# An encoder layer on one core: the Strassen-type down product in visits of half the K-chunks, with its loads and stores spread over three queues

## The chip, the cores and the metric

The program runs on one core of a Trainium2 chip. The metric is the device time of one execution in microseconds; of several executions the median is taken. One more execution was taken with the hardware profiler, and every duration below comes from that one.

## What is computed

One encoder layer is applied to a prompt of 512 rows and a sample of 2,048 rows (2,560 rows of 1,024 floats in the kernel, 20 tiles of 128 rows). The part that matters here is the end of the layer: the gated MLP with its convolution, and the last layer norm.

```python
def conv_gated_mlp(x, w_up, conv_w, conv_b, w_down):
    h = x @ w_up
    ...
    h = h_prev * conv_w[0] + h * conv_w[1] + h_next * conv_w[2] + conv_b
    a, gate = jnp.split(h, 2, axis=-1)
    return (jax.nn.silu(gate) * a) @ w_down

def encoder_trunk(...):
    ...
        x = layer_norm(DEEPNORM_ALPHA * x + mix, ln1_g[l], ln1_b[l])
        f = conv_gated_mlp(x, w_up[l], conv_w[l], conv_b[l], w_down[l])
        x = layer_norm(DEEPNORM_ALPHA * x + f, ln2_g[l], ln2_b[l])
    return x
```

D_FF is 2,816, that is 22 chunks of 128 along the K axis of the down product. Everything is float32; a matrix product is done in three passes over operands that are split into a high and a low part.

## The kernel before, in words

The program has three parts: `project_gla` (names with `front_`), `natten` (`near_`) and `trunk`. The change is in `trunk`, whose own stages follow each other on TensorE: the output projection with the first norm, the up product, and the down product with the last norm. Every engine runs its own list of instructions in order, and a wait on a semaphore holds all that stands behind it on that engine. SyncE (SP) does nothing but ask for DMAs.

**Up product.** It is a Strassen-type product: seven products stand for eight block products. There are 126 steps: six passes over the chunks of W_up (four passes of four lanes, then two of three), in each three blocks of the sequence, in each the seven products. A step is a `phase(n)` of TensorE: four loads of the x operand (`xop`) by every lane, 48 matmuls with four lanes and 36 with three. The result of a lane lies in a PSUM bank, which the step after the next uses again. VectorE reads the banks of products 1, 3, 4, 5, 6 (`take`, L2432), ScalarE those of products 0 and 2 (L2224). In the first steps of each group of seven VectorE also does the convolution of the group before (`convolve_lane`, L2443 and L2450, two lanes a step), ScalarE the centre tap and the silu (L2234, L2241), and GpSimd the product and the store of the gated block g to `g_s` (L2127, L2130).

**The operands of W_down** are made on the way. `CHUNK_TAGS` names for each of 11 chunks (each a pair of K-chunks) the step in which it begins. SyncE loads four quarters of W_down (L1913); in three steps (three, two and two of seven) ScalarE and VectorE write the seven combinations, high half (`emit_hi`, L2264) and low half (`emit_lo`, L2472), into one of two buffers in `trunk_s`, and SyncE stores them to `wop` (`store_emit`, L1918), one after each of its x loads in the step (L1942). GpSimd makes the sums that the combinations need (`combine_down`, L2108 to L2118). The two buffers are the place in which GpSimd also puts a sum of W_up for the next pass (`sum_w`, L2090, L2092); it therefore waits there until all stores of the chunk have landed, and SyncE's loads of the next W_up quarters wait for that sum.

**Down product.** The 20 row tiles are ten pairs; five pairs are one half of the work. A half has seven phases, one for each of the seven products (`DOWN_A`), and in each phase every pair (lane) is visited once: 70 visits in all, each 11 K-chunks of three matmuls with 512 columns, 33 matmuls into the bank of that lane. The right operand of a phase is 11 units of `wop`, 512 KB each, in a ring of 15 (`load_w`, L1951). Its unit comes free when the last lane of the phase has used it, so 15 units mean: the 11 of this phase and 4 of the next. The left operand of a visit is made of blocks of g (704 KB each, rows of 512 bytes; `load_raw`, L1970): one block for most products, three for the product `s2`; `visit_combine` (VectorE, L2484, L2486, L2490) adds or subtracts them, `visit_hi` (ScalarE, L2273) and `visit_lo` (VectorE, L2494) split the result. After a visit VectorE adds the bank to the output rows (`visit_take`, L2507, L2511), and in the last two phases it norms a tile in each visit (`down_norm`, L2521 to L2531; GpSimd stores it, L2161). The rows of x that the result is added to are asked for by `load_rows` (L1979).

All loads of the down product stand in SyncE's list, in the order of the visits:

```python
for v in range(NVISIT):
    while loaded < len(raws) and raws[loaded][0] <= v + 3:
        load_raw(loaded)
        ...
    if v % DLANES == DLANES - 1:
        first = KH * (v // DLANES) + WUNITS
        for u in range(first, min(first + KH, DHALVES * PHASES * KH)):
            load_w(u)
```

and each `load_w` waits there until the last lane has used the unit whose place it takes.

## Time and profile before

| | us |
|---|---|
| median of 3 runs | 3243.07 |
| lowest and highest | 3231.84, 3245.0 |
| the profiled execution, its own time | 3248.93 |
| its span, first to last instruction | 3247.1 |

The span of the profile is 1.8 us shorter than the execution's own time. TensorE is busy for 93% of it, VectorE for 62%, ScalarE for 34%, GpSimd for 22%. A matmul's end is modelled in the profile, so a busy TensorE is not a TensorE at its peak: the number of matmuls in a stretch, times the time that one takes where nothing waits, tells more than the busy time. The DMA share is the mean busy share of the 16 DMA engines; it can come out a little above 1.

### The profile page before, as it was taken

How to read it: one execution, taken by the hardware profiler on the slowest of the kernel's cores; microseconds unless marked ns; L12 is line 12 of the kernel's file. 1: busy time of each engine (PE TensorE's matmuls, PEld its weight loads, DVE VectorE, ACT ScalarE, POOL GpSimd, SP SyncE). 2: the span in 40 equal slices, each digit the busy share in tenths (PEclk: the TensorE clock that was granted, in tenths of full speed). 3: DMA queues.
4: the chain of work that ended last, by engine and by line, in shares of the span. 5: the costliest groups of instructions: out<-in, count | busy, mean ns of one | idle time of the engine just before them, and what ended most of it. 6: DMA issues, size and time to landing. Idle time of an engine off the chain costs nothing.

```text
span 3247.1 us, 42991 instructions
## 1 busy us (share of the span) xinstructions
PE 3016.5 (93%) x15590; PEld 2547.6 (78%) x15590; DVE 2024.5 (62%) x3237; ACT 1102.2 (34%) x2019; POOL 706.1 (22%) x626
## 2 busy tenths in 40 slices
PE   6999999896999998999999999999989988999897
PEld 5777767664777777888899999999879876777685
DVE  7637646743766765668577575775656644466438
ACT  2257346521443442224243332433333321212111
POOL 0012111005445400422333243332333210000000
PEclk9999999987999999999999999999999989999998
DMA  7889788947887766998888888898899989879884
GB/s 279 319 280 305 247 279 264 293 157 256 271 269 234 261 202 207 319 318 296 292 263 314 305 299 308 268 317 303 299 336 355 341 308 302 273 259 335 281 254 148
DMA packets 498946, 910.18 MB, mean 280 GB/s; under 512 B 39952, under 2 KB 274592, under 8 KB 498736
## 3 DMA queue, kind: packets, MB, share of 16 engines
q1 hardware_dynamic: 486096, 854.39, 78.8%
q0 software_dynamic: 12640, 53.04, 4.4%
q8 instruction: 126, 2.06, 0.3%
q14 instruction: 84, 0.69, 0.1%
HBM read 695.85 MB, written 215.55 MB: 281 GB/s over the span
## 4 chain that ended last, share of the span: by engine, by line
PE 36%; DMA 12%; DVE 9%; issue 2%; POOL 1%; ACT 1%; SPq 1%; POOLq 0%; DVEq 0%; ACTq 0%
PE trunk_ps L76 12%; PE trunk_ps L77 12%; PE trunk_ps L78 12%; DMA wop<-trunk_s 3%; DMA shared_spare<-g_s 3%; DMA shared_ring<-xop 2%; DMA trunk_x1t<-g_s 2%; DVE trunk_tt L2443 2%; DVE trunk_tt L2450 1%; DVE shared_ring L2494 1%; DVE trunk_s L2472 1%; DVE trunk_x1t L2484 1%; DVE trunk_x1t L2486 1%; DVE trunk_h L2358 0%; SPq L1970 0%
## 5 line engine op out<-in xcount | busy, mean ns | idle before, releaser
L76 PE MATMUL trunk_ps<-shared_ring 128*128 128x512 f32 (+2 forms) x1202 | 456.5, 380 | 27.5 <-DVE shared_ring L2494 9.3
L77 PE MATMUL trunk_ps<-shared_ring 128*128 128x512 f32 (+2 forms) x1202 | 450.6, 375 | 0.0
L78 PE MATMUL trunk_ps<-shared_ring 128*128 128x512 f32 (+2 forms) x1202 | 448.9, 373 | 0.0
L76 PEld LDWEIGHTS trunk_ps<-shared_ring 128*128 128x128 f32 x1202 | 228.6, 190 | 67.5 <-DMA shared_ring<-wop 16.8
L76 PE MATMUL front_acc<-shared_ring 128*128 128x512 f32 x640 | 260.8, 407 | 8.1 <-ACT front_out L578 8.1
L76 PE MATMUL trunk_ps<-shared_ring,trunk_w_more 128*128 128x426 f32 (+1 forms) x648 | 237.8, 367 | 30.4 <-DMA shared_ring<-xop 30.4
L77 PE MATMUL front_acc<-shared_ring 128*128 128x512 f32 x640 | 252.8, 395 | 0.0
L78 PE MATMUL front_acc<-shared_ring 128*128 128x512 f32 x640 | 252.6, 395 | 0.0
L78 PEld LDWEIGHTS trunk_ps<-shared_ring 128*128 128x128 f32 x1202 | 229.3, 191 | 26.0
L77 PEld LDWEIGHTS trunk_ps<-shared_ring 128*128 128x128 f32 x1202 | 229.2, 191 | 23.8
L76 PE MATMUL trunk_ps<-trunk_w_rest,shared_ring 128*128 128x512 f32 x560 | 223.1, 398 | 25.2 <-DMA trunk_w_rest<-wop 15.3
L77 PE MATMUL trunk_ps<-shared_ring,trunk_w_more 128*128 128x426 f32 (+1 forms) x648 | 236.7, 365 | 0.0
L78 PE MATMUL trunk_ps<-shared_ring,trunk_w_more 128*128 128x426 f32 (+1 forms) x648 | 235.1, 363 | 0.0
L78 PE MATMUL trunk_ps<-trunk_w_rest,shared_ring 128*128 128x512 f32 x560 | 221.5, 396 | 0.0
L77 PE MATMUL trunk_ps<-trunk_w_rest,shared_ring 128*128 128x512 f32 x560 | 221.3, 395 | 0.0
L2127 POOL TENSOR_TENSOR trunk_h<-trunk_tt 128x851 f32<-128x851 f32 (+2 forms) x66 | 130.1, 1971 | 408.1 <-DVE trunk_h L2457 184.7
L2234 ACT ACTIVATE trunk_tt<-trunk_h,trunk_cw 128x851 f32<-128x851 f32 (+2 forms) x132 | 136.4, 1095 | 211.0 <-DVE trunk_h L2432 184.1
L2443 DVE SCALAR_TENSOR_TENSOR trunk_tt<-trunk_h,trunk_cw,trunk_tt 128x851 f32<-128x851 f32 (+3 forms) x176 | 202.0, 1199 | 5.6 <-ACT trunk_tt L2234 4.7
L76 PE MATMUL trunk_ps<-shared_ring,trunk_w_rest 128*128 128x426 f32 (+1 forms) x528 | 191.0, 362 | 12.5 <-DMA shared_ring<-xop 6.9
L77 PE MATMUL trunk_ps<-shared_ring,trunk_w_rest 128*128 128x426 f32 (+1 forms) x528 | 191.3, 362 | 0.0
L78 PE MATMUL trunk_ps<-shared_ring,trunk_w_rest 128*128 128x426 f32 (+1 forms) x528 | 190.0, 360 | 0.0
L2432 DVE TENSOR_TENSOR trunk_h<-trunk_ps,trunk_p 128x426 f32<-128x426 f32 (+1 forms) x198 | 110.6, 598 | 98.1 <-PE trunk_ps L78 97.2
(252 smaller groups left out, 6237.6 us busy)
## 6 DMA issues: line engine op xcount, KB each, us to landing
shared_ring<-xt_s SPq DMA_DIRECT2D x280, 512.0 KB, 6.3
shared_ring<-xop SPq DMA_DIRECT2D x312, 426.0 KB, 5.7
shared_ring<-xop SPq DMA_DIRECT2D x168, 428.0 KB, 5.6
shared_spare<-in_w_up SPq DMA_DIRECT2D x198, 256.0 KB, 5.5
trunk_w_rest<-wop SPq DMA_DIRECT2D x80, 512.0 KB, 8.4
wop<-trunk_s SPq DMA_DIRECT2D x77, 512.0 KB, 5.3
shared_ring<-wop SPq DMA_DIRECT2D x74, 512.0 KB, 9.4
shared_spare<-g_s SPq DMA_DIRECT2D x46, 704.0 KB, 10.2
```

The source lines that it names most:

```text
L76: pe.matmul(out, lh, rh, start=first, stop=False, skip_group_check=skip)
L77: pe.matmul(out, lh, rl, start=False, stop=False, skip_group_check=skip)
L78: return pe.matmul(out, ll, rh, start=False, stop=last, skip_group_check=skip)
L2127: pool.tensor_tensor(part, tt[:, k % 2, 0, 0:n], tt[:, k % 2, 1, 0:n], ALU.mult).then_inc(g_done, 1)
L2234: act.activation(tt[:, k % 2, f, 0:n], h[:, l, f, c:c + n], ACT.Identity, bias=tap[:, 3:4], scale=tap[:, 1:2]).then_inc(tt_done, 1)
L2432: dve.tensor_tensor(out, src, other, ALU.add).then_inc(dve_read, 1)
L2443: ins = dve.scalar_tensor_tensor(out, h[:, l, f, c - 1 + a:c - 1 + b], taps[f][:, 0:1], out, ALU.mult, ALU.add)
L2450: ins = dve.scalar_tensor_tensor(out, h[:, l, f, c + 1 + a:c + 1 + b], taps[f][:, 2:3], out, ALU.mult, ALU.add)
L2472: dve.tensor_tensor(out[:, HALF:D].bitcast(F32R), quad_of(quad_no), out[:, 0:HALF], ALU.subtract).then_inc(wd_lo, 1)
L2484: dve.tensor_tensor(total, raw_a(own[0]), raw_a(own[1]), ALU.add).then_inc(a_comb, 1)
L2486: dve.tensor_tensor(total, total, raw_a(own[2]), ALU.subtract).then_inc(a_comb, 1)
L2494: dve.tensor_tensor(a_buf(v)[:, 1], a_source(v), a_buf(v)[:, 0].bitcast(F32), ALU.subtract).then_inc(a_lo, 1)
```

## The change

A visit is cut in two: the first covers six K-chunks (`KSPAN`), the second five. All five lanes do their first visit, then all five their second; the bank of each lane stays open in between. There are 140 visits, of 18 and of 15 matmuls. A half block of g is 384 or 320 KB; the buffers for it are eight halves in place of four whole ones, and those for the split operand six halves in place of three whole ones. For `a11` both blocks of the first row are loaded and their difference is left in the lane's sum, so that `s2` needs one block more and not three: eight blocks a pair in place of nine.

SyncE's list keeps the loads of x, of W_up, of W_down and of `wop`, and the g halves of the first ten visits; `load_raw` for later visits is in ScalarE's list, `load_rows` in GpSimd's, and `store_emit` in ScalarE's. The chunks that began in steps 9, 30, 51, 72, 93 and 114 begin one step sooner.

```diff
-CHUNK_TAGS = (9, 25, 30, 46, 51, 67, 72, 88, 93, 109, 114)
-DLANES, DHALVES, WUNITS, ABUFS, RAWA = 5, 2, 15, 3, 4
+CHUNK_TAGS = (8, 25, 29, 46, 50, 67, 71, 88, 92, 109, 113)
+KSPAN = ((0, 6), (6, 11))
+DLANES, DHALVES, WUNITS, ABUFS, RAWA = 5, 2, 15, 6, 8
...
-        blocks = {"a11": ((0, 0),), "a12": ((1, 0),), "s2": ((0, 1), (1, 1), (0, 0)), "s3": ((1, 1),), "a22": ((1, 1),),
+        blocks = {"a11": ((0, 0), (0, 1)), "a12": ((1, 0),), "s2": ((1, 1),), "s3": ((1, 1),), "a22": ((1, 1),),
                   "s1": ((0, 0),), "s4": ((1, 0),)}[op]
...
         @block.sync
...
-                    if 1 <= j <= len(emits_at(n)):
-                        store_emit(emits_at(n)[j - 1])
...
+            for r in range(4, RAWA):
+                load_raw(sp, r)
+            for r in range(RAWA, raws_by_sync):
+                load_raw(sp, r)
+            for u in range(WUNITS, DHALVES * PHASES * KH):
+                load_w(u)
...
         @block.gpsimd
             for n in range(NSTEP_UP + 3):
+                c, step = chunk_step(n)
+                if n == NSTEP_UP:
+                    for i in range(2):
+                        pool.wait_ge(wd_stored[i], 16 * len(range(i, PHASES * KH, 2)))
+                    load_rows(pool, 0, 0)
+                    pool.wait_ge(dve_read, len(dve_no))
+                    load_rows(pool, 0, 1)
+                if c is not None:
+                    combine_down(c, step)
                 products(n)
...
-                c, step = chunk_step(n)
-                if c is not None:
-                    combine_down(c, step)
...
+            for l in range(2, DLANES):
+                load_rows(pool, 0, l)
...
         @block.scalar
+            def store_emit(number):
+                c, e, _, out = emit_of(number)
+                act.wait_ge(wd_lo, number + 1)
+                act.dma_start(wop[DOWN_W.index(EMITS[e]), c], out).then_inc(wd_stored[number % 2], 16)
+
+            def emits(n):
+                numbers = emits_at(n)
+                for j, number in enumerate(numbers):
+                    emit_hi(number)
+                    if j:
+                        store_emit(number - 1)
+                if numbers:
+                    store_emit(numbers[-1])
...
             for v in range(1, NVISIT + 1):
-                if 3 <= v + 2 < NVISIT:
-                    visit_hi(v + 2)
+                if 8 <= v + 5 < NVISIT:
+                    visit_hi(v + 5)
+                while loaded < len(raws) and raws[loaded][0] <= v + 10 and raws[loaded - RAWA][0] <= v + 3:
+                    load_raw(act, loaded)
+                    loaded += 1
...
         @block.vector
+            take(NSTEP_UP - 1)
+            visit_combine(0)
+            visit_combine(1)
+            visit_lo(2)
+            visit_lo(3)
+            visit_combine(2)
+            visit_combine(3)
+            convolve_lane(LAST_S, 0)
+            visit_lo(4)
+            visit_combine(4)
+            convolve_lane(LAST_S, 1)
...
             for v in range(1, NVISIT + 1):
-                if 3 <= v + 2 < NVISIT:
-                    visit_lo(v + 2)
+                if 8 <= v + 5 < NVISIT:
+                    visit_lo(v + 5)
                 visit_take(v - 1)
-                if v + 3 < NVISIT:
-                    visit_combine(v + 3)
+                if 7 <= v + 6 < NVISIT:
+                    visit_combine(v + 6)
...
         @block.tensor
-                for k in range(KH):
-                    u = KH * (v // DLANES) + k
+                k0, k1 = KSPAN[g]
+                for k in range(k0, k1):
+                    u = KH * (v // PER_PHASE) + k
```

**First place: SyncE around the first chunk of W_down.** The rows are DMA requests in the order of SyncE's list; `wop<-trunk_s` is a store of a W_down operand, `shared_ring<-xop` loads of x for the up product, `shared_spare<-in_w_up` quarters of W_up. Before:

```order
L1918 DMA wop<-trunk_s 128x1024
L1942 DMA shared_ring<-xop 128x852 x3
L1913 DMA shared_spare<-in_w_up 128x512 x6
L1918 DMA wop<-trunk_s 128x1024
L1942 DMA shared_ring<-xop 128x852
L1918 DMA wop<-trunk_s 128x1024
L1942 DMA shared_ring<-xop 128x852 x3
L1913 DMA shared_spare<-in_w_up 128x512 x6
```

With the change, the same stretch from the load of the four W_down quarters on:

```order
L1966 DMA shared_spare<-in_w_down 128x512 x4
L1990 DMA shared_ring<-xop 128x852 x16
L1966 DMA shared_spare<-in_w_up 128x512 x6
L1990 DMA shared_ring<-xop 128x852 x4
L1966 DMA shared_spare<-in_w_up 128x512 x6
```

The stores are gone from SyncE's list; between the quarters of W_down and the first six of W_up now stand 16 loads of x, that is four steps.

**Second place: VectorE around the same chunk.** L2457 (L2500 with the change) ends a lane of the convolution, `trunk_s<-shared_spare,trunk_s` writes the low half of a W_down operand, and `trunk_h<-trunk_ps,trunk_p` reads four banks of a step. Before:

```order
L2450 SCALAR_TENSOR_TENSOR trunk_tt<-trunk_h,trunk_cw,trunk_tt 128x851 x2
L2457 COPY trunk_h<-trunk_h 128x2x2
L2432 TENSOR_TENSOR trunk_h<-trunk_ps,trunk_p 128x426 x4
L2472 TENSOR_TENSOR trunk_s<-shared_spare,trunk_s 128x512 x5
L2432 TENSOR_TENSOR trunk_h<-trunk_ps,trunk_p 128x426 x4
L2472 TENSOR_TENSOR trunk_s<-shared_spare,trunk_s 128x512 x2
```

With the change:

```order
L2493 SCALAR_TENSOR_TENSOR trunk_tt<-trunk_h,trunk_cw,trunk_tt 128x851 x2
L2500 COPY trunk_h<-trunk_h 128x2x2
L2515 TENSOR_TENSOR trunk_s<-shared_spare,trunk_s 128x512 x3
L2475 TENSOR_TENSOR trunk_h<-trunk_ps,trunk_p 128x426 x4
L2515 TENSOR_TENSOR trunk_s<-shared_spare,trunk_s 128x512 x4
L2475 TENSOR_TENSOR trunk_h<-trunk_ps,trunk_p 128x426 x4
```

Three low halves have moved ahead of the read of the four banks that follows the convolution.

**Third place: the requests of the down product.** `g_s` is the gated block, `wop` the operands of W_down. Before, all in SyncE's list:

```order
L1951 DMA trunk_w_rest<-wop 128x1024 x4
L1951 DMA shared_ring<-wop 128x1024 x7
L1970 DMA trunk_x1t<-g_s 128x11x128
L1970 DMA shared_spare<-g_s 128x11x128 x2
L1970 DMA trunk_x1t<-g_s 128x11x128 x2
```

With the change, in ScalarE's list, between the high halves of the left operand:

```order
L2302 ACTIVATE shared_ring<-shared_spare 128x640
L1901 DMA trunk_x1t<-g_s 128x6x128 x2
L2302 ACTIVATE shared_ring<-trunk_x1t 128x768
L1901 DMA shared_spare<-g_s 128x6x128
L1901 DMA shared_spare<-g_s 128x5x128
```

SyncE's list has only loads of `wop` after the first ten visits' g, and ScalarE asks for g one or two halves at a time.

## Rows read from the trace of the kernel before

**Rows 1.** The page, its head.
```profile
span 3247.1 us, 42991 instructions
```

**Rows 2.** Busy time by stretch, up product; columns stand in the first line.
```profile
core 0: us, PE busy (x) PEld busy (x) DVE busy (x) ACT busy (x) POOL busy (x), PEclk, DMA share, GB/s
...
1598.10:1624.60 26.50, 21.20 (x98) 19.77 (x98) 5.00 (x9) 2.25 (x3) 10.17 (x8) 0.88 0.86 307
1624.60:1802.70 178.10, 178.10 (x914) 172.35 (x913) 130.74 (x174) 69.94 (x100) 59.17 (x44) 1.00 0.88 297
1802.70:1828.60 25.90, 21.21 (x97) 19.76 (x96) 4.97 (x9) 2.23 (x3) 10.19 (x8) 0.89 0.86 309
2016.60:2042.90 26.30, 21.70 (x97) 20.47 (x97) 12.46 (x15) 6.42 (x8) 12.12 (x10) 0.87 0.72 227
2221.10:2232.90 11.80, 9.63 (x50) 9.02 (x49) 2.37 (x5) 0.82 (x1) 6.93 (x6) 1.00 0.78 279
...
2368.80:2419.20 50.40, 38.44 (x181) 34.83 (x181) 16.69 (x25) 6.70 (x12) 16.53 (x14) 0.97 0.92 333
...
2496.70:2569.50 72.80, 67.14 (x325) 61.70 (x323) 39.15 (x57) 20.39 (x30) 19.07 (x14) 0.98 0.99 360
...
2598.00:2636.70 38.70, 32.39 (x146) 29.30 (x144) 5.33 (x9) 1.69 (x3) 0.00 (x0) 0.91 1.02 387
```

**Rows 3.** The same view, down product: visits 0-14, 15-29, 30-49, 50-69.
```profile
2636.70:2782.70 146.00, 124.26 (x495) 97.21 (x496) 77.99 (x81) 30.03 (x26) 8.39 (x6) 0.93 0.88 273
2782.70:2894.90 112.20, 112.20 (x496) 92.94 (x496) 57.92 (x54) 22.15 (x18) 1.07 (x2) 1.00 0.80 253
2894.90:3074.50 179.60, 161.04 (x661) 126.00 (x661) 105.48 (x111) 29.55 (x29) 4.26 (x8) 0.95 0.95 307
3074.50:3225.50 151.00, 150.37 (x661) 123.46 (x659) 95.53 (x101) 27.75 (x27) 4.04 (x8) 1.00 0.71 233
```

**Rows 4.** Waits of TensorE, 2636.7 to 3225.5: total us, times, longest.
```profile
PE trunk_ps L76 <- DVE shared_ring L2494: 19.2, 7, 5.0
PE trunk_ps L76 <- DMA trunk_w_rest<-wop: 15.3, 7, 6.3
PE trunk_ps L76 <- DMA shared_ring<-wop: 6.2, 20, 0.4
```

**Rows 5.** Waits before 2640: GpSimd's, then SyncE's queue.
```profile
POOL shared_spare L2090 <- DMA wop<-trunk_s: 88.6, 5, 18.9
...
SPq L1913 <- POOL trunk_s L2092: 36.8, 8, 7.2
```

**Rows 6.** Timeline of SyncE, 1601 to 1625: start, us, what.
```profile
1600.22 2.69 SPq L1942 DMA_DIRECT2D shared_ring<-xop  x3
1609.92 3.89 SPq L1913 DMA_DIRECT2D shared_spare<-in_w_up  x6
```

**Rows 7.** Timeline of VectorE, step 29: last lane of the convolution, then bank read.
```profile
1772.62 3.58 DVE L2443 SCALAR_TENSOR_TENSOR trunk_tt<-trunk_h,trunk_cw,trunk_tt 128x851 f32<-128x851 f32 x2
...
1778.37 2.13 DVE L2432 TENSOR_TENSOR trunk_h<-trunk_ps,trunk_p 128x426 f32<-128x426 f32 x4
```

**Rows 8.** DMA issues of the page: count, KB, median us to landing.
```profile
wop<-trunk_s SPq DMA_DIRECT2D x77, 512.0 KB, 5.3
...
shared_spare<-g_s SPq DMA_DIRECT2D x46, 704.0 KB, 10.2
```

**Rows 9.** The chain that ended last, 2560 on: start, us, what.
```profile
2738.90 7.87 SPq L1970
```

**Rows 10.** Timeline of VectorE at the end: bank reads of visits 64, 65, 68, 69.
```profile
3199.41 0.68 DVE L2511 TENSOR_TENSOR trunk_tt<-trunk_tt,trunk_ps 128x512 f32<-128x512 f32 x1
...
3207.24 0.68 DVE L2511 TENSOR_TENSOR trunk_s<-trunk_s,trunk_ps 128x512 f32<-128x512 f32 x1
...
3224.81 0.68 DVE L2511 TENSOR_TENSOR trunk_h<-trunk_h,trunk_ps 128x512 f32<-128x512 f32 x1
...
3229.69 0.68 DVE L2511 TENSOR_TENSOR trunk_tt<-trunk_tt,trunk_ps 128x512 f32<-128x512 f32 x1
```

261 lines of the change are left out of this document (138 added, 123 removed).

## The prediction

> **What bounds the kernel now.** I read the page first, then busy time by stretch, then TensorE's waits, then the queues of the engines that it waits for. The span [rows 1] is TensorE's: the stretches in which nothing waits show it without a gap, at a granted clock of 1.00, the upper of its two levels (2.4 GHz; the lower is 1.2). So I count what each stretch loses against that pace.
>
> In the up product the quiet stretch 1624.6 to 1802.7 holds 914 matmuls in 178.1 us, 0.195 us each [rows 2]. Around the chunks that begin in steps 9, 30, 51 and 72 the stretches of 26.5, 25.9, 26.3 and 11.8 us hold 98, 97, 97 and 50 matmuls, 19.1, 18.9, 18.9 and 9.8 us of work [rows 2]: 7.4 + 7.0 + 7.4 + 2.0 = 23.8 us lost. The reason is a queue. GpSimd waits 88.6 us in five waits for the stores of W_down operands to land before it may sum W_up in the same buffers, and SyncE waits 36.8 us for those sums [rows 5]. While SyncE stands at such a W_up quarter, the x loads behind it are not asked for: after the requests that begin at 1600.22 it issues nothing until 1609.92 [rows 6].
>
> The last up stretches are another case. Where the passes have three lanes, the share of the DMA engines is 0.92 in 2368.8 to 2419.2, 0.99 in 2496.7 to 2569.5 and 1.02 in the last 38.7 us [rows 2].
>
> In the down product 15 undisturbed visits take 112.2 us, 7.48 each [rows 3]; 70 would take 523.6. The four stretches [rows 3] take 146.0, 112.2, 179.6 and 151.0 us for 15, 15, 20 and 20 visits: 33.8 + 0 + 30.0 + 1.4 = 65.2 us lost. Waits are 19.2 + 15.3 + 6.2 = 40.7 us of it [rows 4]; the other 24.5 lie in the lower clock, since the granted clock is 0.93 and 0.95 in just the stretches that have the waits and 1.00 in the others [rows 3]. The losses come where both lists are heaviest: at the start, at the change of half, and at `s2`. SyncE's queue has a share: the chain holds 7.87 us in which a load of g waited in it [rows 9], behind a W unit whose place was in use.
>
> **The change part by part.** The sum is made against the profiled execution, whose span is that of [rows 1] and whose own time, 3248.9 us, lies 5.9 above the median of the runs.
>
> *Visits of half the K-chunks, and loads in separate lists.* A first visit takes 18/33 of 7.48, 4.08 us, a second 3.40; the sum of matmuls is unchanged, and visits follow each other without a seam in [rows 3]. Six W units come free after 20.4 us of a phase and five at its end, so a unit is asked for 20 us or more before it is used; the 21.5 us of waits for W [rows 4] go. SyncE's W waits hold no g any more, and g is asked for ten visits ahead, some 37 us, against a landing time of 10.2 us for a block twice as large [rows 8]. All 65.2 us of loss can go; what is late next is the following.
>
> *The start, 20 us back.* Only 8 half blocks are in place before the up product ends. VectorE must then do the last bank read, three convolution lanes (a lane of step 29 took 5.75 us, from 1772.62 to the bank read at 1778.37 [rows 7]), six low halves and seven sums at 0.75 us each: 5.75 × 3 + 2 + 13 × 0.75 = 29 us beside the 30.6 us of the first eight visits. With the waits for g between them that leaves 3.5 us of gaps. Then g for visits 10 and 11 is asked for when W's first units and GpSimd's row loads are: six W units and eight rows or gain vectors of 512 KB each are 7.3 MB, some 19 us at the 387 GB/s of the last up stretch [rows 2], beside what g itself needs. VectorE's read of bank 5 stands behind the low halves of visits 10 and 11 in its list, and visit 10 needs that bank. I put 9 us of wait there, the 3.5 at visits 4 and 5, and 7.5 for the lower clock after them (24.5 us for 40.7 of waits before, 0.6 for one). Bounds: 8, if g lands as fast as alone, and 34, what the stretch loses now.
>
> *The change of half, 7 us back.* In the last two phases VectorE norms a tile in each second visit: the spacing of its reads is 4.88 us with the norm alone (3224.81 to 3229.69) and 7.83 with a low half and a sum of full length (3199.41 to 3207.24) [rows 10], so a second visit costs VectorE 4.88 + 1.6 = 6.5 us against 3.4 of TensorE, a first one 1.4 to 1.6 against 4.08. It falls behind by 15 us in five visits; six operand buffers are 20 us of cover. ScalarE's requests for g stand behind its square roots, which follow VectorE, so the lead of 37 us shrinks to some 10 just where `a11` needs two blocks and rows go out and in. Between 0 and 30, what it loses now, I take 7, near the lower end, since the buffers still cover the lag.
>
> *The tail, 4 us more.* VectorE now reads bank 69 at 3229.69, 4.2 us after the last visit ended at 3225.5 [rows 3, 10], and needs 4.9 for that tile. With second visits of 3.40 it enters the last five reads about 2 us late and does 5 × 4.88 = 24.4 us of work against 13.6 of TensorE's that remain: it ends 12.6 us after TensorE in place of 9.1. The same stores follow.
>
> *Stores by ScalarE, one step sooner.* With a step between the last operand and the sum, the stores (5.3 us to landing [rows 8]) are in before GpSimd asks: the 23.8 us go. But the chunk now begins in the step in which VectorE convolves lanes 2 and 3. Its first three low halves stand ahead of the read of the step's four banks, which came at 1778.37, right behind the convolution [rows 7]. The third waits for a store to land: 0.7 + 5.3 + 1.3 = 7.3 us, so the read moves to about 1785.7; TensorE needs the bank at 1783.9, two steps of 48 × 0.195 = 9.4 us before step 33, which begins at 1802.7 [rows 2]. That is 1.8 us and 1.1 in the clock; GpSimd's sums of the chunk come sooner too, and I take half, 1.5 us for each of the four, 6; bounds 0 and 17, the whole for all six chunks that move. ScalarE holds its own list until each low half is written; its next bank read comes some 3 us later and still in time.
>
> *Three-lane passes, 5 us gained.* The stretch 2368.8 to 2419.2 has 50.4 us for 181 matmuls, 35.3 us of work: 15.1 lost, with a DMA share of 0.92 [rows 2]. So 4 us of idle DMA are there, and 1 in the later chunk. GpSimd asks for the first rows before the up product ends; 1 MB at 387 GB/s is 2.6 us in a stretch that is full at 1.02 [rows 2], and I count them as lost. Splitting VectorE's operations in two adds a fixed part to each, but outside the two places above VectorE has 57.92 us busy in 112.20 [rows 3], so I cost it at nothing; it would show as a longer tail if that cover were gone.
>
> Sum: 3248.9 − 65.2 + 20 + 7 + 4 − 23.8 + 6 − 5 + 2.6 = 3194.5, that is 54.4 less; on the median of 3243.1 it is 3188.7, so **3189 us**.
>
> **A rule beside it.** At step 12 the DMA share is 0.86 while TensorE loses 7.4 us [rows 2]: the DMA engines had room, and it was SyncE's list that waited; in 2496.7 to 2569.5 the share is 0.99, and there they had none. The Trainium skill, "DMA: Bandwidth & Descriptors", section "Issuing engines are not separate DMA queues", says that requests from different engines end on the same 16 DMA engines, and that spreading them saves only the issuing time. By that rule, the second stretch agrees and the first does not, since a list that is held by a wait is more than issuing time. It speaks against this change, and what it would make of the time is the first rival.
>
> **The rivals.**
> 1. *The DMA engines set the pace*: what no longer waits in a list waits for the data. For: shares of 0.88 and 0.95 in the two bad down stretches [rows 3]. From the quiet one (0.80 of 112.2 us for 33 W units and 15 blocks, W at 387 GB/s 1.36 us each) a block takes 3.0 us; a half then needs 40 × 3.0 + 77 × 1.36 + 20 × 1.36 = 252 us of DMA against 262 of TensorE, and before, with 45 blocks, 267. At the 0.88 of the first stretch, 507 us for both halves and the gains become 576, 52 over 523.6. Then only 13 of the 65.2 are gained, the three-lane passes give nothing, and the time is 3248.9 − 13 + 4 − 23.8 + 6 + 2.6 = 3225, or 3219 on the median. Against: 0.95 was reached over 180 us.
> 2. *It goes better*: the start loses 10, the change of half nothing, the three-lane passes give 10 and no bank read is late: 3248.9 − 65.2 + 10 + 4 − 23.8 − 10 + 2.6 = 3166.5, or 3161. For: ten visits of lead; against: VectorE's list above.
> 3. *Slower: operands made in the wrong step.* ScalarE now waits for a low half and for its own store's landing in all 33 steps that make operands. If each of them holds a bank read for the 7.3 us above, against 5.5 to spare, TensorE waits 1.8 us and loses 1.1 in the clock in each: 33 × 2.9 = 96 in place of the 6, so 3194.5 + 90 = 3284, or 3279 on the median. It decides from 1.8 us a step, where it takes all 60. Against: in five of the eleven chunks the step is the one before the change, with no convolution ahead of it, and only the first of a chunk's three steps puts its halves ahead of a read that TensorE needs at once.
>
> **How the numbers follow.** Forecast 0.63 (between 3170 and 3210), the DMA engines 0.14, better 0.17, slower 0.04, and 0.02 for a mishap that leaves it where it is. A measurement of this kernel can tell 0.5%, 16 us, from no change, so faster means under 3227: the forecast, the better case and most of rival 1, 0.91; 0.05 stays within; slower 0.04. The range from 3160 to 3220 takes in the better case's value and rival 1's.
>
> **What would show it.** Right: stretches around steps 12, 33 and 54 at 0.195 us a matmul; no wait for `wop`; down waits left only near 2650 to 2700 and at the half, for VectorE's low halves; VectorE ending some 12 us after TensorE. Wrong in a step: bank reads of the step after the convolution on TensorE's wait list with over 3 us each; a loss at the change of half as large as before; gaps in visits of the middle phases, which would mean that g or W is late in the steady state and would break the forecast.

## The result and the profile after

The changed kernel takes 3223.7 us (median of 8 runs, 3216.4 to 3227.4) against 3243.0 before (8 runs, 3231.8 to 3253.5): a ratio of 0.994, with an interval of 0.9923 to 0.9956. It is faster, by 19 us and not by 54; the time lies 3.7 us above the range. The first line of the page of the changed kernel stands beside [rows 1]:

```profile
span 3221.3 us, 43444 instructions
```

Its own time is 3223.1 us, 25.8 less than the profiled execution of before. Busy time by stretch says where that came from. First the up product of the kernel before, its four-lane and its three-lane passes:

```profile
core 0: us, PE busy (x) PEld busy (x) DVE busy (x) ACT busy (x) POOL busy (x), PEclk, DMA share, GB/s
1478.50:2298.40 819.90, 799.03 (x4043) 769.06 (x4041) 550.05 (x717) 292.58 (x419) 268.10 (x201) 0.99 0.86 294
2298.40:2636.70 338.30, 309.79 (x1513) 289.88 (x1512) 197.88 (x273) 107.43 (x149) 96.35 (x72) 0.97 0.96 345
```

Then the changed kernel: the same two stretches, and the down product in four, half visits 0 to 19, 20 to 67, 68 to 83 and 84 to 139:

```profile
1473.20:2272.90 799.70, 791.34 (x4044) 762.70 (x4042) 550.81 (x717) 292.17 (x419) 274.90 (x201) 1.00 0.89 301
2272.90:2623.60 350.70, 313.12 (x1513) 297.11 (x1512) 203.37 (x274) 107.58 (x150) 98.14 (x74) 0.94 0.93 336
...
2623.60:2722.60 99.00, 80.97 (x332) 64.97 (x331) 65.54 (x89) 26.80 (x32) 13.49 (x16) 0.90 0.91 289
2722.60:2902.80 180.20, 180.20 (x796) 149.21 (x796) 101.11 (x133) 38.49 (x52) 2.67 (x5) 1.00 0.79 263
2902.80:2985.80 83.00, 67.11 (x268) 53.78 (x268) 54.52 (x77) 15.19 (x23) 7.93 (x15) 0.90 1.02 327
2985.80:3194.10 208.30, 208.27 (x919) 172.11 (x917) 122.08 (x161) 41.91 (x58) 3.21 (x7) 1.00 0.67 223
```

| stretch | before | after | difference | forecast |
|---|---|---|---|---|
| up to the up product | 1478.5 | 1473.2 | −5.3 | 0 |
| four-lane passes | 819.9 | 799.7 | −20.2 | −17.8 |
| three-lane passes | 338.3 | 350.7 | +12.4 | −2.4 |
| down product | 588.8 | 570.5 | −18.3 | −38.2 |
| behind TensorE's last matmul | 21.6 | 27.2 | +5.6 | +4 |

The first line is not the change's: no code ahead of the up product differs, and in the thirteen profiles of kernels with the change (that of this section and those of the runs below) the up product begins anywhere between 1468.6 and 1477.7.

The long middle stretches of the down product have no wait and the upper clock (1.00, that is 2.4 GHz). Their 180.2 us for 795 matmuls are 0.2267 us each, so 74.8 us would do for the first 20 half visits (330 matmuls) and 60.5 for the 16 at the change of half (267). They take 99.0 and 83.0: **24.2 and 22.5 us are lost**, where the prediction had 20 and 7. TensorE's waits in the down product, for [rows 4]:

```profile
PE trunk_ps L76 <- DVE shared_ring L2538: 14.5, 4, 9.9
PE trunk_ps L76 <- issue: 11.4, 1, 11.4
PE trunk_ps L76 <- DVE trunk_h L2556: 4.1, 2, 2.2
PE trunk_ps L76 <- DVE trunk_p L2552: 2.0, 1, 2.0
PE trunk_ps L76 <- DVE trunk_tt L2556: 1.9, 1, 1.9
```

No wait for `wop` is left of the 21.5 us of [rows 4]. Two single waits carry most: 11.4 us, which end at 2680.9, and 9.9, which end at 2960.3.

**At the start** the first long wait stands behind ScalarE. Its timeline from 2660 on (start, us, what; ACTq is its queue's issue of DMAs):

```profile
2660.67 6.42 ACTq L1901 DMA_DIRECT2D trunk_x1t<-g_s  x2
2668.32 0.85 ACT L2302 ACTIVATE shared_ring<-trunk_x1t 128x768 fp32r<-128x768 f32 x1 [7.00 <-DMA trunk_x1t<-g_s]
2668.39 8.67 ACTq L1901 DMA_DIRECT2D shared_spare<-g_s  x2
2677.16 0.84 ACT L2302 ACTIVATE shared_ring<-trunk_x1t 128x768 fp32r<-128x768 f32 x1 [7.99 <-issue]
2677.24 8.12 ACTq L1901 DMA_DIRECT2D shared_spare<-g_s  x1
2685.47 0.85 ACT L2302 ACTIVATE shared_ring<-trunk_x1t 128x768 fp32r<-128x768 f32 x1 [7.46 <-issue]
```

These are the high halves of visits 10, 11 and 12. The g of visits 11 and 12 had landed at 2669.6 and 2670.9, by the trace's DMA records. ScalarE came to them 7.6 and 14.6 us later, since the requests for visits ahead stand between them in its list, and one such request now takes 8 us to issue. VectorE's low halves and, behind them, its bank reads follow ScalarE, and TensorE follows those. The g of visit 13, asked for at 2664.5, landed only at 2685.0, so that the next bank read would have come late all the same.

**What makes a load of g late to land,** the packets of each queue show; why its request is slow to issue they do not show. In 2671 to 2683 of the changed kernel (q0 is GpSimd's queue, with rows of x; q1 SyncE's, with W; q10 ScalarE's, with g):

```profile
q0 software_dynamic: 655, 2.39, 49.3%
q1 hardware_dynamic: 588, 2.14, 44.5%
q10 hardware_dynamic: 661, 0.33, 9.7%
issues: line engine op xcount, KB each, median us to landing
shared_spare<-g_s ACTq DMA_DIRECT2D x2, 320.0 KB, 18.5
```

While all three queues have work, each has about the same *number* of packets served. A packet of g has 512 bytes and one of W or of a row some 4096, so g gets 0.33 of 4.86 MB, and 320 KB of it take 18.5 us. At the change of half the counts are equal too while all three have work, here in 2945 to 2952:

```profile
q0 software_dynamic: 364, 1.36, 47.7%
q1 hardware_dynamic: 367, 1.33, 46.5%
q10 hardware_dynamic: 363, 0.18, 8.6%
```

The halves of g for visits 78 and 79 are on the way then (the window of this line is 2936 to 2960):

```profile
shared_spare<-g_s ACTq DMA_DIRECT2D x4, 320.0 KB, 20.9
```

These four were asked for at 2936.5 to 2940.8 and landed at 2952.7 to 2960.9. TensorE is ready for visit 78 at 2950.5 and waits 9.9 us for its low half. ScalarE's and VectorE's timelines show two reasons:

```profile
2953.04 0.74 ACT L2302 ACTIVATE shared_ring<-shared_spare 128x640 fp32r<-128x640 f32 x1 [14.67 <-DMA shared_spare<-g_s]
...
2958.72 0.82 DVE L2528 TENSOR_TENSOR trunk_x1t<-shared_spare 128x640 f32<-128x640 f32 x1 [17.48 <-DMA shared_spare<-g_s]
2959.47 0.82 DVE L2538 TENSOR_TENSOR shared_ring<-shared_spare,shared_ring 128x640 fp32r<-128x640 f32 x1
```

The high half follows the first block, which landed at 2952.7. But in VectorE's list the difference that `a11` leaves for `s2` (L2528) stands ahead of the low half (L2538), and it needs the second block, which landed at 2958.6. Some 6 us of the 9.9 are thus the order of VectorE's list (an estimate: the low half could have begun at 2953.8 and began at 2959.5), though visit 79, whose first block landed at 2959.8, would then have waited instead. No run changed that order. Another 6.0 us in three waits, ahead of visits 72 to 74, are VectorE's bank reads behind its norms (the L2556 of the list above). The prediction had 10.2 us for a block twice that size [rows 8]. The Trainium skill, "DMA: Bandwidth & Descriptors", section "Queues, rings and completion order", says that each DMA engine goes round the queues that have work, at the granularity of a packet. The counts above agree with it, where a packet is one row of 512 or 4096 bytes.

**In the three-lane passes** the largest losses sit in two steps, 94 and 115, with single waits of 8.09 and 9.15 us. ScalarE's and VectorE's timelines ahead of the first:

```profile
2354.94 0.33 ACTq L2285 DMA_DIRECT2D wop<-trunk_s  x1
2360.36 0.63 ACT L2280 ACTIVATE trunk_s<-shared_spare 128x512 fp32r<-128x512 f32 x1 [10.97 <-DMA wop<-trunk_s]
...
2361.02 0.69 DVE L2515 TENSOR_TENSOR trunk_s<-shared_spare,trunk_s 128x512 fp32r<-128x512 f32 x1 [5.51 <-ACT trunk_s L2280]
2361.63 1.61 DVE L2475 TENSOR_TENSOR trunk_h<-trunk_ps,trunk_p 128x426 f32<-128x426 f32 x3
```

The first operand is stored at 2354.94; the third may be written into its place when that store has landed, at 2360.36; its low half follows, and only then VectorE reads the bank for which TensorE waits until 2362.37.

### The profile page after: what moved, and what is told of

It reads as the page before. It is cut to its first block, busy times and chain, and to the rows that moved or that the text cites. A ratio compares the mean times of both kernels' runs of the same rounds, so it can differ in the third digit from the quotient of the medians.

```text
span 3221.3 us, 43444 instructions
## 1 busy us (share of the span) xinstructions
PE 2997.0 (93%) x15590; PEld 2545.5 (79%) x15590; DVE 2041.3 (63%) x3357; ACT 1113.8 (35%) x2089; POOL 725.1 (23%) x648
## 4 chain that ended last, share of the span: by engine, by line
PE 39%; DVE 11%; DMA 7%; issue 2%; ACT 1%; POOL 1%; ACTq 1%; SPq 0%; DVEq 0%; POOLq 0%
PE trunk_ps L76 13%; PE trunk_ps L77 13%; PE trunk_ps L78 13%; DMA wop<-trunk_s 3%; DVE trunk_tt L2486 2%; DVE trunk_tt L2493 2%; DMA shared_ring<-xop 2%; DMA shared_spare<-g_s 1%; DMA trunk_x1t<-g_s 1%; DVE trunk_stats L2566 1%; DVE trunk_s L2515 1%; ACTq L1901 1%; DVE trunk_h L2401 0%; DVE shared_ring L2538 0%; PE trunk_ps L2670 0%
## 5 line engine op out<-in xcount | busy, mean ns | idle before, releaser
L76 PE MATMUL trunk_ps<-shared_ring 128*128 128x512 f32 (+2 forms) x1202 | 452.4, 376 | 23.8 <-PEq L1072 5.4
L77 PEld LDWEIGHTS trunk_ps<-shared_ring 128*128 128x128 f32 x1202 | 228.1, 190 | 24.4
L76 PE MATMUL trunk_ps<-trunk_w_rest,shared_ring 128*128 128x512 f32 x560 | 221.0, 395 | 23.3 <-issue 11.4
L76 PE MATMUL trunk_ps<-shared_ring,trunk_w_more 128*128 128x426 f32 (+1 forms) x648 | 233.0, 360 | 7.7 <-DMA shared_ring<-xop 7.7
L77 PE MATMUL trunk_ps<-shared_ring,trunk_w_more 128*128 128x426 f32 (+1 forms) x648 | 233.6, 360 | 0.0
L78 PE MATMUL trunk_ps<-shared_ring,trunk_w_more 128*128 128x426 f32 (+1 forms) x648 | 232.1, 358 | 0.0
L76 PE MATMUL trunk_ps<-shared_ring,trunk_w_rest 128*128 128x426 f32 (+1 forms) x528 | 194.5, 368 | 30.4 <-DVE trunk_h L2475 20.1
L2486 DVE SCALAR_TENSOR_TENSOR trunk_tt<-trunk_h,trunk_cw,trunk_tt 128x851 f32<-128x851 f32 (+3 forms) x176 | 194.7, 1158 | 2.9 <-ACT trunk_tt L2250 2.1
L77 PE MATMUL trunk_ps<-shared_ring,trunk_w_rest 128*128 128x426 f32 (+1 forms) x528 | 194.1, 368 | 0.0
L78 PE MATMUL trunk_ps<-shared_ring,trunk_w_rest 128*128 128x426 f32 (+1 forms) x528 | 192.6, 365 | 0.0
L2515 DVE TENSOR_TENSOR trunk_s<-shared_spare,trunk_s 128x512 fp32r<-128x512 f32 x77 | 67.7, 895 | 169.2 <-ACT trunk_s L2280 169.1
```

Source lines behind the costliest of these rows:

```text
L76: pe.matmul(out, lh, rh, start=first, stop=False, skip_group_check=skip)
L77: pe.matmul(out, lh, rl, start=False, stop=False, skip_group_check=skip)
L78: return pe.matmul(out, ll, rh, start=False, stop=last, skip_group_check=skip)
L2486: ins = dve.scalar_tensor_tensor(out, h[:, l, f, c - 1 + a:c - 1 + b], taps[f][:, 0:1], out, ALU.mult, ALU.add)
L2515: dve.tensor_tensor(out[:, HALF:D].bitcast(F32R), quad_of(quad_no), out[:, 0:HALF], ALU.subtract).then_inc(wd_lo, 1)
```

## The experiments

All edits are of the changed kernel. The theories are lettered as in the expectations: for the three-lane passes A, an engine's bank read stands behind a third operand that waits for a store to land, against B, the DMA engines are full; for the down product P, g starves by equal turns of packets, and Q, ScalarE is held by its own requests, against C, the requests are late, and against the first rival's bytes. Each ratio is to the kernel before, run on the same chip; a 95% interval stands in brackets. This table has the lengths of the stretches of each profile in us, bounded as above.

| run | four-lane | three-lane | start | change of half | median us | ratio |
|---|---|---|---|---|---|---|
| the change | 799.7 | 350.7 | 99.0 | 83.0 | 3223.7 | 0.9940 |
| e1_tags_back | 799.3 | 346.9 | 96.9 | 84.5 | 3223.1 | 0.9930 |
| e2_two_first | 803.7 | 346.9 | 96.8 | 82.6 | 3223.3 | 0.9934 |
| e3_ask_sooner | 802.0 | 350.2 | 100.4 | 77.0 | 3224.0 | 0.9928 |
| e4_long_packets | 802.3 | 349.2 | 90.3 | 77.7 | 3207.1 | 0.9886 |
| e5_sync_asks | 803.6 | 346.2 | 94.1 | 73.2 | 3206.3 | 0.9880 |
| e6_four_steps | 811.0 | 344.1 | 97.6 | 82.8 | 3227.9 | 0.9947 |
| e7_tile_layout | 814.1 | 351.8 | 90.9 | 78.5 | 3210.8 | 0.9900 |
| e8_gains_later | 801.2 | 347.0 | 99.4 | 82.9 | 3221.4 | 0.9928 |
| e9_sync_w_first | 799.7 | 346.8 | 89.1 | 71.4 | 3202.4 | 0.9876 |
| e10_four_last | 799.2 | 344.7 | 99.8 | 82.3 | 3212.5 | 0.9908 |
| e11_both | 801.7 | 343.7 | 87.7 | 71.8 | 3199.9 | 0.9864 |
| e12_gpsimd_asks | 800.0 | 346.3 | 94.9 | 84.4 | 3211.8 | 0.9894 |

Kernels whose edit lies in the down product alone (e3, e4, e5, e8, e9, e12) have 346.2 to 350.2 us in the three-lane passes, which no line of them touches: a difference of 4 us there says nothing. With the change they are seven profiles of the same code, 348.1 us in the mean, 9.8 above the one profile of the kernel before. In the same way the runs whose edit lies in the up product alone (e1, e2, e6, e10) have 96.8 to 99.8 us at the start and 82.3 to 84.5 at the change of half.

### The three-lane passes

**e1_tags_back**: the two last tags as before.

```diff
-CHUNK_TAGS = (8, 25, 29, 46, 50, 67, 71, 88, 92, 109, 113)
+CHUNK_TAGS = (8, 25, 29, 46, 50, 67, 71, 88, 93, 109, 114)
```

> Of the changed kernel only the chunk tags 92 and 113 go back to 93 and 114; the four other tags that moved stay one step sooner. Theory A (a bank read behind a low half): in steps 92 and 113 VectorE's read of product 1 stands behind the third low half, which waits for a store to land; the gaps of 8.09 and 9.15 us on TensorE at 2362 and 2530 go, with the clock after them 10.6 + 11.65 us, and what comes back is the loss of the kernel before in the same 42 steps, so that they take about 338 us in place of 350.8: 12 us less, 3212. Theory B (the DMA engines are full in the three-lane passes): which step begins a chunk makes no difference; the stretch stays near 350 us and the time at 3224, within 4.

Measured: 3223.1, ratio 0.9930 [0.9916, 0.9943]; no gain that can be told from the change. Both named waits are gone, and others stand in their place: in 2355 to 2390 TensorE waits 3.07 us for VectorE's read, 4.15 for *ScalarE's* bank read and 6.77 for an x load. The third operand holds whichever engine has a bank to read behind it. With the old tags the stretch is still 8.6 us longer than before the change, when SyncE made the stores; so the tags alone are not what costs.

**e2_two_first**: two operands, then three.

```diff
-                    return [PHASES * c + e for e in range(*EMIT_AT[n - tag])]
+                    return [PHASES * c + e for e in range(*(EMIT_EARLY if tag % PHASES == 1 else EMIT_AT)[n - tag])]
+EMIT_EARLY = ((0, 2), (2, 5), (5, 7))
```

> The tags of the changed kernel stay. In the six chunks that begin one step sooner the first step makes two of the seven operands and the second three, in place of three and two. The two buffers are then both free in the first step and no low half ahead of the bank read waits for a store. Theory A: the gaps of 8.09 and 9.15 us go and with them 22 us of loss; the four-lane passes stay at 800 us; 3202 to 3208. Theory B (the DMA engines): nothing changes, 3224 within 4, and TensorE waits in the same steps for x loads in place of bank reads.

Measured: 3223.3, ratio 0.9934 [0.9919, 0.9948]; a miss of the same kind. In the first chunk's steps the 8.09 us became 3.71 for VectorE's read and 3.67 for ScalarE's. In the whole of the three-lane passes ScalarE's reads held TensorE twice in each of the two runs, for 9.3 us in e1 and 8.5 in e2.

**e6_four_steps**: two, two, two, one, for every chunk.

```diff
-EMIT_AT = ((0, 3), (3, 5), (5, 7))
+EMIT_AT = ((0, 2), (2, 4), (4, 6), (6, 7))
```

> A chunk's seven operands of W_down are made in four steps, two, two, two and one, in place of three, two and two; the tags of the changed kernel stay. No operand of a step then waits for the store of another of the same step. Theory A, widened by the runs before (whichever engine stands behind a third operand that waits for a store to land: VectorE's bank read in the changed kernel, ScalarE's bank read with the tags back): the waits for VectorE's and for ScalarE's bank reads in the three-lane passes, 17.6 us in the changed kernel, go under 4; what stays is the wait for x loads; the 42 steps take 335 to 342 us in place of 350.8, 3209 to 3215. Theory B (the DMA engines): the waits only turn into waits for x loads, the 42 steps stay at 347 to 351, 3224 within 4.

Measured: 3227.9, ratio 0.9947 [0.9936, 0.9959]. Half of theory A came out: no wait for a bank read is left in the three-lane passes. But the wait moved once more, to x loads, 10.58 us in step 92 and 10.14 in step 113. SyncE's waits in 2340 to 2370 say why (who waits, for whom: total us, times, longest):

```profile
SPq L1990 <- PE trunk_ps L78: 11.7, 5, 6.0
SPq L1966 <- DVE trunk_s L2515: 11.7, 1, 11.7
```

A quarter of W_down for the chunk of step 92 waits for its place, which the chunk before frees a step later than it did; the x loads stand behind it. Not the DMA engines but a third engine's list was held. In the four-lane passes the edit cost 11.3 us more, which the expectation had left out: there too SyncE waits longer for such a place, 36.8 us in place of 10.8, and TensorE 9.9 us for x loads in place of 0.8.

**e10_four_last**: four steps for the chunks of steps 92 and 113 alone.

```diff
+EMIT_LATE = ((0, 2), (2, 4), (4, 6), (6, 7))
+def emits_of(tag):
+    return EMIT_LATE if tag in (92, 113) else EMIT_AT
```

> The changed kernel, with four steps (two, two, two and one operands) for the two chunks alone that begin in steps 92 and 113; all others keep three. In the run with four steps for every chunk SyncE stood 11.7 us at a quarter of W_down, whose place came free a step later since the chunk of steps 88 to 91 ended where that of 92 begins; here it ends in step 90. Theory A: neither VectorE's nor ScalarE's bank reads are waited for in the three-lane passes, and SyncE isn't held: the 42 steps take 334 to 341 us in place of 350.8, 3208 to 3214. Theory B (the DMA engines are full): 346 to 351 us, with waits for x loads in place of the others; 3220 to 3225.

Measured: 3212.5, ratio 0.9908 [0.9893, 0.9923]. The time is within theory A's range; the stretch of 344.7 us lies between the two expectations. It is 6.0 us shorter than the change's and 1.5 shorter than the shortest of the profiles with unchanged three-lane passes, so it accounts for 1.5 to 6 of the 11 us between the medians; where the rest lies was not found. TensorE's waits in the three-lane passes, first of the kernel before, then of the change, then of this run (each has one more wait, of 3.5 us, that ends with nothing that the profile shows):

```profile
PE trunk_ps L76 <- DMA shared_ring<-xop: 24.9, 21, 3.8
```

```profile
PE trunk_ps L76 <- DVE trunk_h L2475: 17.6, 3, 9.2
PE trunk_ps L76 <- DMA shared_ring<-xop: 16.5, 10, 4.2
```

```profile
PE trunk_ps L76 <- DMA shared_ring<-xop: 20.0, 8, 6.2
PE trunk_ps L76 <- DVE trunk_h L2482: 8.7, 4, 3.8
```

The waits for bank reads are halved, but 3.5 us came back as waits for x loads. Both theories hold in part: A named the wait, and B's x loads take over some of what A's edit frees.

### The down product

**e3_ask_sooner**: one visit more of lead.

```diff
-                while loaded < len(raws) and raws[loaded][0] <= v + 10 and raws[loaded - RAWA][0] <= v + 3:
+                while loaded < len(raws) and raws[loaded][0] <= v + 11 and raws[loaded - RAWA][0] <= v + 4:
```

> ScalarE asks for each half block of g one visit sooner (both limits of its loop raised by one), otherwise the changed kernel. Theory C (the requests are late, since they stand behind ScalarE's square roots that wait for VectorE): at the change of half the requests go out about 6.5 us sooner, their time to land falls from a median of 20.9 us towards 10, the gap of 9.88 us at the read of visit 75 (2960.3) falls under 4; 3215. Theory P (packets: g's packets of 512 bytes get one turn in three beside packets of 4096 bytes in the two other queues): the landing time stays at 16 us or more, as there are just as many bytes of W and rows beside it; what is gained is at most the 6.5 us, and the gap of 11.45 us at the start (2680.9) stays; 3217 to 3222.

Measured: 3224.0, ratio 0.9928 [0.9913, 0.9943]; within noise of the change. The wait at the change of half fell from 9.88 to 6.84 us and that stretch by 6.0; the wait at the start is 7.98 with others around it, that stretch no shorter. One visit of lead is thus worth 6.0 of the 22.5 us at the change of half and nothing at the start; theory C holds for that part. In e5 and e9 below the requests there go out sooner still.

**e4_long_packets**: the same bytes, longer rows.

```diff
-            eng.dma_start(raw_place(r).rearrange("p (k n) -> p k n", n=P),
-                          g_s[k0:k1, :, rows_of(2 * pair + row)].rearrange("k p n -> p k n")).then_inc(ra_in[r % RAWA], 16)
+            at = min((2 * pair + row) * P, TOK - width)
+            eng.dma_start(raw_place(r), g_s[kh * KH + KSPAN[g][0], :, at:at + width]).then_inc(ra_in[r % RAWA], 16)
```

> A half block of g is read from one K-chunk's rows, 3072 or 2560 bytes in a row in each partition, in place of six or five times 512 bytes: the same bytes from the same tensor, but other values of g, so the down product's result is not the reference's. Theory P: the DMA engines take a packet from each busy queue in turn, so that a load with packets of 3 KB gets six times the bytes at each turn; the requests at the start and at the change of half land in under 10 us in place of 16 to 22, the gaps of 11.45 us at 2680.9 and 9.88 us at 2960.3 go with their clock, 15 to 25 us less: 3199 to 3209. Theory of the DMA engines' bytes (the first rival of the prediction): the same bytes take the same time and the down product stays at 570 us, 3224 within 5. Theory C (late requests): the requests go out when they did; the gap at 2960.3 falls by no more than the shorter transfer alone, and 3217 or more.

Measured: 3207.1, ratio 0.9886 [0.9870, 0.9903]. The start lost 8.7 us of its length, the change of half 5.3. In both stretches no request of ScalarE takes longer than 1.2 us to issue, and at the start ScalarE begins the high halves of visits 10 to 13 within 3.2 us, from 2669.46 to 2672.69. The same bytes in fewer packets are 14 us faster, so the bytes alone do not set the pace. Since the edit shortens the landing and frees ScalarE's list at once, it does not tell P from Q. But at the change of half most requests still took 11 to 13 us to land (medians), and of the loss 90.3 − 74.8 = 15.5 and 77.7 − 60.5 = 17.2 us remain.

**e5_sync_asks**: the requests back in SyncE's list, ordered with W.

```diff
         @block.sync
...
+            loaded = raws_by_sync
+            for v in range(1, NVISIT + 1):
+                while loaded < len(raws) and raws[loaded][0] <= v + 10 and raws[loaded - RAWA][0] <= v + 3:
+                    load_raw(sp, loaded)
+                    loaded += 1
+                for u in range(WUNITS, DHALVES * PHASES * KH):
+                    phase, k = divmod(u - WUNITS, KH)
+                    if v == phase * PER_PHASE + (DLANES if k < KSPAN[0][1] else 2 * DLANES):
+                        load_w(u)
...
         @block.scalar
...
-                while loaded < len(raws) and raws[loaded][0] <= v + 10 and raws[loaded - RAWA][0] <= v + 3:
-                    load_raw(act, loaded)
-                    loaded += 1
```

> The requests for g of visits 10 and later go back to SyncE's list, in which they stand among the W units in the order in which both come due (six units after five visits, five after ten); nothing else of the changed kernel moves, and g keeps its packets of 512 bytes. Theory Q (ScalarE is held by its own requests: in the trace of the changed kernel one request takes 8.2 us to issue, from 2668.85 to 2677.06, while g of visit 11 has landed at 2669.6, and its high half starts at 2677.16): the gap of 11.45 us at 2680.9 falls under 4, the start gets some 10 us shorter, and the change of half keeps most of its 9.88, since there the blocks landed late and not only the high halves; 3212 to 3216. Theory P (packets of g starve beside packets of 4096 bytes in other queues): g and W are now in one queue in the order of the requests, g waits for W's burst in front of it; the start stays within 4 us, the change of half gets worse or stays; 3220 to 3230.

Measured: 3206.3, ratio 0.9880 [0.9867, 0.9893], better than either theory had. The start is only 4.9 us shorter, since W's first burst now stood behind six more requests for g (2658.1 to 2664.4; with those of visits 8 and 9 ten) and TensorE waited 9.57 us for a unit. The g of visits 10 to 13, asked for ahead of that burst in the same queue, landed after 4.6 to 6.8 us. The change of half, where theory Q expected little, is 9.8 us shorter. The landing is no faster there: the halves for visits 78 and 79 took 19.0 to 23.8 us. But SyncE, which waits for no square root, asked for them 20 to 27 us after the stretch begins, ScalarE in the change only after 34 to 38. So the gain there came with the earlier request, as theory C has it.

**e9_sync_w_first**: the same, with W's first burst ahead of g.

```diff
+            for u in range(WUNITS, WUNITS + KSPAN[0][1]):
+                load_w(u)
             loaded = raws_by_sync
```

> As the run in which SyncE asks for g, but the first six W units of the second phase are asked for ahead of g of visits 10 and later (there they stood behind ten requests for g and landed at 2680 to 2688; TensorE waited 9.57 us for one). Theory Q: ScalarE is free as before, g of visits 10 to 13 lands by 2668 and W by 2668, and the start has no wait over 4 us left: the first 20 half visits take 86 to 89 us in place of 94.1 (99.0 in the changed kernel, 75.1 if nothing waited), 3199 to 3202. Theory P (sharing by packets): with W's burst ahead in the same queue, g of visit 10 lands after 2675 and TensorE waits 8 us or more for VectorE's low half as in the changed kernel; 3205 or more.

Measured: 3202.4, ratio 0.9876 [0.9862, 0.9891]; the start is at 89.1, at the upper edge of what Q had. Its start and its change of half:

```profile
2624.20:2713.30 89.10, 81.06 (x332) 65.31 (x331) 65.50 (x89) 26.95 (x33) 13.50 (x16) 0.92 1.00 315
...
2893.50:2964.90 71.40, 63.89 (x269) 50.80 (x268) 53.16 (x76) 14.25 (x22) 7.95 (x15) 0.98 1.08 361
```

The losses are 89.1 − 74.8 = 14.3 and 71.4 − 60.5 = 10.9, 25.2 us in place of 46.7, with g still in packets of 512 bytes. ScalarE's timeline now has the high halves of visits 10 to 13 in a row, each right behind its landing (the first and the last are shown):

```profile
2668.24 0.85 ACT L2311 ACTIVATE shared_ring<-trunk_x1t 128x768 fp32r<-128x768 f32 x1 [10.46 <-DMA trunk_x1t<-g_s]
...
2672.22 0.84 ACT L2311 ACTIVATE shared_ring<-trunk_x1t 128x768 fp32r<-128x768 f32 x1 [0.43 <-DMA trunk_x1t<-g_s]
```

The g of visit 13 landed at 2672.2, where it was 2685.0 in the change: the second burst of W, asked for at 2666.8 to 2669.5 there, stands behind g here and goes out from 2685.9 on.

At the change of half the halves for visits 78 and 79, asked for in 2913 to 2921, land no faster than the 20.9 us of the change:

```profile
shared_spare<-g_s SPq DMA_DIRECT2D x4, 320.0 KB, 20.0
```

But they are asked for 20 to 27 us after the stretch begins, as in e5, and TensorE, which comes to visit 78 at 2936.4, waits about 1 us. What helps there is the earlier request, not a shorter landing.

The equal turns are still there where two queues are full. In 2672 to 2682 of this run, rows in q0 against g in q1:

```profile
q0 software_dynamic: 968, 3.52, 87.8%
q1 hardware_dynamic: 926, 0.47, 15.8%
```

Here two halves of g took 15 us to land, and one request took SyncE 6.5 us to issue, from 2673.91 to 2680.44; but nothing that computes stands behind it. The turns are not equal everywhere: in 2928 to 2940 of this run, again rows against g, q0 has 879 packets and q1 2700. Why is open.

**e12_gpsimd_asks**: g and rows change places.

```diff
         @block.gpsimd
...
-            for l in range(2, DLANES):
-                load_rows(pool, 0, l)
+                while loaded < len(raws) and raws[loaded][0] <= v + 10 and raws[loaded - RAWA][0] <= v + 3:
+                    load_raw(pool, loaded)
+                    loaded += 1
...
         @block.scalar
...
-                    load_raw(act, loaded)
+                    for l in range(2, DLANES):
+                        load_rows(act, 0, l)
```

> g and rows change places, otherwise the changed kernel: GpSimd asks for g of visits 10 and later, ScalarE for the rows of three of the five lanes and for the last norm's vectors. There are still three queues, of which one holds packets of 512 bytes, and the same bytes; but the engine that asks for g computes nothing in the down product, and a request for rows has few packets. Theory Q (ScalarE held by its own requests): as in the run in which SyncE asks, the high half of visit 11 starts when its g has landed; the first 20 half visits take 88 to 94 us in place of 99.0. Theory P (equal turns by packets starve g, whoever asks): g of visits 14 and 15 lands 18 us after its request as in the changed kernel and the first 20 half visits take 97 to 101, the 16 at the change of half 80 to 85 (83.0 in the changed kernel, 71.4 with SyncE asking).

Measured: 3211.8, ratio 0.9894 [0.9878, 0.9911]; start 94.9, just outside Q's 88 to 94, change of half 84.4. It does not test what it was made for. The queues in 2671 to 2683:

```profile
q10 hardware_dynamic: 412, 1.49, 38.2%
q1 hardware_dynamic: 414, 1.50, 32.4%
q0 software_dynamic: 410, 1.40, 31.8%
```

A packet of g that GpSimd asks for has 1.40 MB / 410 = 3.4 KB in the mean, not 512 bytes (by the trace's records 341 of 4096 bytes and 69 of 4). So this is a third case of equal turns, now with equal bytes, and not a test of short packets. ScalarE's first high half came at 2664.97, held by the wait that its own requests for rows needed. The change of half did not gain: GpSimd's requests stand there behind its stores, which wait for norms, and those for visits 78 and 79 go out 40 to 43 us after the stretch begins, later than ScalarE's in the change, and land after 12 to 17 us.

Most of the gain lies elsewhere. This profile is 14.4 us shorter than the change's. Of that 2.7 lie in the down product, now 567.8 us, 4.4 in the three-lane passes, which the edit does not touch, and 6.8 behind TensorE's last matmul, 20.4 us in place of 27.2. GpSimd's closing DRAIN is the reason there, first of the change, then of this run (ns, least, median and most, then the start):

```profile
L1598 POOLq DRAIN  x1: 9123/9123/9123, 3212.0 to 3212.0; - x1
```

```profile
L1598 POOLq DRAIN  x1: 2266/2266/2266, 3204.4 to 3204.4; - x1
```

Neither theory had this, and what the DRAIN waits for is open.

**e7_tile_layout**: g in longer rows, by another layout of the tensor.

```diff
-    xop, g_s = scratch("xop", NSB, PHASES, P, 2 * 4 * NMAX), scratch("g_s", FC, P, TOK)
+    xop, g_s = scratch("xop", NSB, PHASES, P, 2 * 4 * NMAX), scratch("g_s", NT, P, FC * P)
...
-                pool.dma_start(g_s[PASSES[s // NSB][l], :, a:b], part).then_inc(g_stored[l], 16)
+                for t0, t1, c0, c1 in g_parts(a, b):
+                    pool.dma_start(g_s[t0:t1, :, at + c0:at + c1].rearrange("t p n -> p t n"),
...
+            eng.dma_start(raw_place(r), g_s[2 * pair + row, :, k0 * P:k1 * P]).then_inc(ra_in[r % RAWA], 16)
```

> g is stored by row tiles (20 tiles of 128 partitions with 22 chunks of 128 floats in a row), so that a half block is read with 3072 or 2560 bytes in a row; the store of a gated block is cut into two or three requests, with 512 bytes in a row or less where it had 3408. All values are the reference's. Theories P and Q: the down product becomes that of the run with long packets, 557 us in place of 570; the price is in the up product, 66 blocks with six times as many packets: at the 28 ns that a packet of 512 bytes takes against some 130 for one of 3408, about 0.3 us more for each block on the 16 engines, 20 us of transfers that hide in the four-lane passes and cost up to 5 in the three-lane ones; 3208 to 3214. Theory B (bytes, not packets): the gain in the run with long packets came from something else in it (a different part of the tensor), and here nothing is gained: 3224 or slower.

Measured: 3210.8, ratio 0.9900 [0.9885, 0.9916]. The down product is 557.9 us, as in e4 (556.5), so the gain there is the packets' and not that of the part of the tensor which e4 read. The four-lane passes took 814.1, 14.4 more than the change's: the cost of short stores did not hide there, as the expectation had said it would. Against that, GpSimd's closing DRAIN takes 4.2 us in place of 9.1, which the expectation did not have either; so that the time lies in its range is in part luck. The profile is the slowest of the kernel's six runs, 3223.6; how much the stores cost in the others is not shown.

**e8_gains_later**: the two vectors of the last norm later.

```diff
+            pool.wait_ge(d_read, read_by[25])
             pool.dma_start(gain2, ln2_g.partition_broadcast(P)).then_inc(gain2_in, 16)
```

> GpSimd asks for the last norm's two vectors (1 MB) only after visit 25 in place of right behind the first rows; otherwise the changed kernel. If bytes in GpSimd's queue hold back g at the start (P, and the first rival), 1 MB less of 5 MB between 2666 and 2690 shortens the start by 2 to 4 us; if ScalarE's held requests alone set it (Q), the queue drains sooner too, with the same 2 to 4. If VectorE's list sets the start (the prediction's view), nothing changes. 3219 to 3224.

Measured: 3221.4, ratio 0.9928 [0.9915, 0.9941]; start 99.4, change of half 82.9: nothing. By the expectation that speaks for the prediction's view, but the trace says otherwise. The g of visits 12 and 13 landed at 2664.3 and 2672.8, after 10.1 and 15.0 us in place of 10.2 and 20.6, so the landing did get shorter. ScalarE did not come to them, since one request took 12.2 us to issue:

```profile
2664.61 12.17 ACTq L1901 DMA_DIRECT2D shared_spare<-g_s  x1
2676.89 0.84 ACT L2303 ACTIVATE shared_ring<-trunk_x1t 128x768 fp32r<-128x768 f32 x1 [11.51 <-issue]
```

TensorE's wait of 11.4 us became two of 5.2 and 6.6. The second is ScalarE's list alone, as theory Q says.

**e11_both**: e9 and e10 together.

> Both edits at once: SyncE asks for g with W's first burst ahead, and the chunks of steps 92 and 113 take four steps. If the two losses are of different stages they add up: under theories Q and A 3199 to 3202 less some 12, 3186 to 3191, about the prediction's 3189; under P and B 3205 to 3225.

Measured: 3199.9 (3193.5 to 3201.4), ratio 0.9864 [0.9847, 0.9880]: the fastest of the runs, 1.4% below the kernel before. The start is 87.7, the change of half 71.8, the three-lane passes 343.7. Against e9 the second edit gives 2.5 us and not 12; the single times of the two runs overlap (e9 3199.3 to 3206.2).

## Why the prediction was wrong

The direction was right, and so was the bound (below 3227). The order of the parts was not: the four-lane passes gained more than the down product. By its steps:

- **Stores and the four-lane passes: right.** −17.8 forecast, −20.2 measured. TensorE's waits for x loads there fell from 16.8 us to 0.8. The late bank read costs less than the 1.5 us a chunk: there are four such waits of 0.95 us at most, 2.9 in all.
- **W and the middle of a half: right.** No wait for `wop`; the half visits 20 to 67 follow each other without a gap, as do those from 84 on.
- **The tail: right**, +5.6 for +4. VectorE ends 14.4 us after TensorE, at 3208.4, where 12.6 was forecast (by its own terms 2 + 24.4 − 13.6 is 12.8).
- **The three-lane passes: wrong, −2.4 forecast, +12.4 measured.** The step that failed is "5.5 to spare". That a third low half waits for a landing was foreseen, at 7.3 us; from store to bank read it is 6.7. But the spare time was taken from four-lane steps (48 × 0.195 = 9.4 us), and the sum has the cost for the four chunks in those passes alone; a three-lane step is 36 × 0.195 = 7.0 us. There nothing was to spare: VectorE was done with the convolution at 2354.3, and TensorE was ready for the bank at 2362.37 − 8.09 = 2354.3. So the wait came through whole: with the clock that the pauses cost, steps 94 and 115 lost 10.6 and 11.7 us against the 7.0 that they need. A second step was put at nothing and failed too: ScalarE's next bank read, "some 3 us later and still in time", held TensorE for up to 5.2 us in e1 and 4.9 in e2. Whether the gain of 5 from "4 us of idle DMA" came cannot be told: the waits for x loads fell from 24.9 to 16.5 us, but they were 20.0 again in e10, with half of the other waits gone. Four edits moved these waits about; none gave the stretch of before back (344.1 to 346.9 us against 338.3), so what keeps it longer wherever the operands are placed stays open.
- **The start: sized nearly right, in part by luck.** 20 forecast, 24.2 measured. The 3.5 us of VectorE's backlog came (0.88 and 3.44). The 9 us were to be VectorE's read behind low halves that wait for g; g of visits 11 and 12 was there, and ScalarE, which the prediction left out, was not. The late landing that it did expect came one visit later, with g of visit 13.
- **The change of half: wrong, 7 forecast, 22.5 measured.** The step that failed is the landing time: 10.2 us of [rows 8], taken as an upper bound for half the bytes. The halves for visits 78 and 79 took 16 to 22. That row is the median of the whole down product; the blocks of 704 KB that the kernel before asked for in 2895 to 2903 took far longer too:

  ```profile
  shared_spare<-g_s SPq DMA_DIRECT2D x2, 704.0 KB, 17.9
  ```

  The lead was nearly right, "some 10" forecast and 14 measured (asked for at 2936.5, needed at 2950.5). Either a longer lead (e3, e5, e9) or a shorter landing (e4) takes 5 to 12 us of the loss away. VectorE's lag, which "the buffers still cover", was put at nothing and cost 6.0 us of waits.

Of rival 1, the time was nearest (3219), but its mechanism does not explain the 14 and 12.6 us that e4 and e7 gain in the down product with the same bytes. For the 25.2 us that e9 still loses it is not excluded: the DMA engines are busy at 1.00 and 1.08 in its two stretches. The Trainium skill's rule beside it ("DMA: Bandwidth & Descriptors", section "Issuing engines are not separate DMA queues") says that spreading requests over engines saves issuing time alone. The down product does not speak against it: with one list for g and W (e9) it takes 548.9 us, 21.6 less than with two. The four-lane passes do: there stores out of SyncE's list brought 20.2 us, since that list was held by a wait.

Had the loads been ordered as in e9, the down product would have lost 25.2 us, where the prediction allowed 27. The profile of e11, whose own time is 3199.6, is then 5.1 us above the prediction's sum of 3194.5; the three-lane passes have 343.7 us in place of 338.3 − 2.4 = 335.9. It comes near by other terms and is not the forecast come true.

What stays open: how much of the start's loss is ScalarE's held list and how much the slow landing. An estimate from the rows of the change: TensorE went on at 2680.9, 3.7 us after ScalarE had begun the high half of visit 11. Had ScalarE begun it on landing, at 2669.6, TensorE would have gone on at 2673.3, 4 us after it stopped, and would have stood at visit 12 from 2681.5 until 3.7 us after 2685.0, some 7 us. That makes 11 in place of the 13.4 that it waited at visits 10 and 11; so the landing alone would have cost nearly as much. No run kept the three queues and the short packets and freed ScalarE alone. Nor was a third buffer for operands tried, which would take the wait for a landing away without moving it.

## What to carry to other kernels

A load that moves to a queue of its own takes turns with the other queues packet by packet: price it with its own packet size against theirs, and not by a median landing time; take the time that it has where the queues are busiest. Then ask for it by that much ahead: the lead brought more at the change of half than anything else. Requests that may take long to issue belong on an engine that computes nothing and whose list is not held by one that does, in the order in which they are needed. Where a wait is said to fit into spare time, work the spare time out for the shortest step of the program in which it occurs.

## What the runs showed of the hardware

Queues that had work at once got about equal numbers of packets, whatever their size: 655, 588 and 661 in one stretch of three queues, 364, 367 and 363 in another, 968 and 926 in one of two, and 410, 412 and 414 with packets of like size. One stretch of two queues does not fit, with 879 and 2700. A request of g (five or six rows of 512 bytes in each of 128 partitions) took up to 12.2 us to issue from ScalarE, from 2940.76 to 2952.94, with several requests of its kind ahead in the queue, against 0.33 to 1.2 with long rows; ScalarE begins nothing else meanwhile. A load by GpSimd of rows of 512 bytes came out in packets of 4 KB, where ScalarE's and SyncE's had 512 bytes. GpSimd's DRAIN at the end of the program took 9.1 us in the change and in every run with the same number of GpSimd's DMA requests (162), 8.7 in the kernel before (140 requests), 4.2 in e7 (250) and 2.3 in e12 (288); the span ends 0.2 us behind it. What sets its length is not shown.
